# Moving the convolution accumulators of a decoder block into PSUM, and the layer-norm matmuls two gate chunks earlier

## The reference

```python
h  = RMSNorm(x)
u  = h @ w_in        # conv a, conv gate, q, k, v, indexer q, k, weights, branch gates
c  = a * sigmoid(gate)                      # 512 channels
c  = causal_depthwise_conv(c, width=31) + conv_b
c  = silu(LayerNorm(c)) @ w_conv_out        # branch A
y  = sparse_attention(top 256 keys of an indexer, 8 heads, ALiBi) @ w_attn_out   # branch B
x  = x + (sigmoid(g_A) * c + sigmoid(g_B) * y) @ w_out
x  = x + SwiGLU(RMSNorm(x));   out = RMSNorm(x)
```

## Time and profile before

| | us |
|---|---|
| median of 3 runs (lowest, highest) | 3663.2 (3662.07, 3664.06) |
| time of the profiled execution | 3664.39 |
| its span, first to last instruction | 3662.6 |
| PE busy | 3306.2 |
| DVE busy | 2275.9 |
| ACT busy | 1225.0 |
| POOL busy | 717.3 |

### The profile page before, as it was taken

The page is one execution under the profiler, slowest core; times in us unless marked ns, Lnnn a source line. Parts: engine busy times, 40 slices in busy tenths (PEclk is TensorE's granted clock), DMA queues, the critical chain, the costliest instruction groups (busy, mean ns, idle before and its releaser), DMA issues.

```text
span 3662.6 us, 42966 instructions
## 1 busy us (share of the span) xinstructions
PE 3306.2 (90%) x15365; PEld 2699.9 (74%) x15365; DVE 2275.9 (62%) x4000; ACT 1225.0 (33%) x2407; POOL 717.3 (20%) x482
## 2 busy tenths in 40 slices
PE   6971699999998899989999889998999978889998
PEld 5851578768887788758887778875788857768886
DVE  2968735678704935679972973667999988720001
ACT  3321542242334731251112763226211156621111
POOL 3420120026766100002112300000112231002112
PEclk9986799999999999999999999999999989999999
DMA  6951275559996165535555016552555510155554
GB/s 219 309 173 35 104 276 188 191 189 291 290 289 227 65 251 189 180 117 194 195 195 190 24 74 237 194 179 87 184 195 195 199 43 7 59 208 194 195 195 167
DMA packets 177571, 640.20 MB, mean 175 GB/s; under 512 B 11293, under 2 KB 95305, under 8 KB 115560
## 3 DMA queue, kind: packets, MB, share of 16 engines
q1 hardware_dynamic: 160512, 574.66, 45.4%
q10 hardware_dynamic: 16872, 63.01, 4.5%
HBM read 476.14 MB, written 161.48 MB: 174 GB/s over the span
## 4 chain that ended last, share of the span: by engine, by line
PE 62%; DVE 18%; issue 13%; ACT 3%; DMA 2%; POOL 1%; DVEq 0%; ACTq 0%; SPq 0%; POOLq 0%
PE PS L1346 13%; PE PS L1317 12%; PE PS L1319 12%; PE PS L1318 12%; DVE flags L1113 2%; DVE part_max L1200 2%; PE PS L1331 2%; DVE W L1098 1%; PE PS L1332 1%; PE PS L1333 1%; DVE PT L1212 1%; PE PS L1459 1%; PE PS L1504 1%; DVE ties L942 1%; DVE W L1212 1%
## 5 line engine op out<-in xcount | busy, mean ns | idle before, releaser
L1113 DVE TENSOR_SCALAR_CACHE_REDUCE flags<-W,cand 128x1408 uint8<-128x1408 f32 (+3 forms) x462 | 683.4, 1479 | 53.7 <-DVE cand L1143 40.0
L1346 PE MATMUL PS<-WS,HT 128*128 128x512 f32 x2088 | 481.8, 390 | 5.6 <-POOL WS L427 3.3
L1346 PEld LDWEIGHTS PS<-WS,HT 128*128 128x128 f32 x2088 | 392.9, 188 | 88.5 <-issue 4.1
L1317 PE MATMUL PS<-HF,WS 128*128 128x512 f32 x1072 | 419.8, 392 | 16.1 <-issue 13.8
L1318 PE MATMUL PS<-HF,WS 128*128 128x512 f32 x1072 | 419.2, 391 | 0.0
L1319 PE MATMUL PS<-HF,WS 128*128 128x512 f32 x1072 | 419.0, 391 | 0.0
L498 POOL TENSOR_TENSOR TMP<-TMP 128x512 f32<-128x512 f32 x88 | 113.4, 1289 | 1554.7 <-ACT TMP L855 1554.7
L427 POOL TENSOR_TENSOR WS<-RAW,WS 128x1024 fp32r<-128x1024 f32 x116 | 281.5, 2427 | 654.6 <-ACT WS L570 620.5
L1317 PE MATMUL PS<-HT,WS 128*128 128x512 f32 x824 | 325.2, 395 | 0.0
L1319 PE MATMUL PS<-HT,WS 128*128 128x512 f32 x824 | 320.8, 389 | 0.0
L1318 PE MATMUL PS<-HT,WS 128*128 128x512 f32 x824 | 320.6, 389 | 0.0
(11 more groups left out here) (223 smaller groups left out, 6376.5 us busy)
## 6 DMA issues: line engine op xcount, KB each, us to landing
WS<-split_weights_scratch SPq DMA_DIRECT2D x234, 1024.0 KB, 4.8
split_weights_scratch<-WS SPq DMA_DIRECT2D x116, 1024.0 KB, 5.0
W<-split_weights_scratch SPq DMA_DIRECT2D x114, 1024.0 KB, 4.8
RAW<-in_w_in SPq DMA_DIRECT2D x34, 512.0 KB, 6.0
RAW<-in_w_ffn_gate SPq DMA_DIRECT2D x22, 512.0 KB, 6.3
RAW<-in_w_ffn_up SPq DMA_DIRECT2D x22, 512.0 KB, 6.3
RAW<-in_w_ffn_down SPq DMA_DIRECT2D x22, 512.0 KB, 5.7
W<-in_x ACTq DMA_DIRECT2D x4, 2048.0 KB, 12.3
```

The source lines that it names most:

```text
L1113: step(nc.vector.tensor_scalar(flags[:, 0:n], SC[:, t, 0:n], cand[:, t:t + 1].bitcast(f32), 0.0, op, ALU.add, accum_out=count[:, t:t + 1]))
L1317: mm(PS[:, bank, :], wh, src[:, 0, k, :], start=k == 0, stop=False)
L1346: ins = mm(PS[:, 2 * t + half, :], lhs, split(c, w_part)[:, half * 512:(half + 1) * 512], start=first and part == 0 and w_part == 0, stop= ...
```

## The change

The convolution's accumulator of each 128 channels moves from SBUF into one of the PSUM banks 4 to 7 (`TAPSUM`). Only the last tap writes to `ACC` in SBUF. All projections now share banks 0 to 3: queries in a ring of four, gate B in a ring that starts at bank 2, the key/value transposes in banks 2 and 3, gate A in a ring of two (banks 0 and 1), mean and variance in banks 2 and 3. In `taps` and in the first tap (L1018) `ACC` becomes `TAPSUM` in the same way as in `tap`. Waits follow the banks. `LN_MEAN` and `LN_VAR` become 3 and 5, so the two products are issued ahead of gate-A chunks 3 and 5, and ACT's squares and square root come after its gates 2 and 4. The number of instructions does not change.

```diff
-    LN_MEAN, LN_VAR = 5, 7
+    LN_MEAN, LN_VAR = 3, 5
+        TAPSUM = PS[:, 4:8, :]
...
-            def tap(k):
+            def tap(k, out):
...
-                    nc.vector.scalar_tensor_tensor(out=ACC[:, c, :], in0=GLU[:, c, k:k + ROWS], scalar=cw[:, c, k:k + 1],
-                                                   in1=ACC[:, c, :], op0=ALU.mult, op1=ALU.add).then_inc(conv_step, 1)
+                    nc.vector.scalar_tensor_tensor(out=out[:, c, :], in0=GLU[:, c, k:k + ROWS], scalar=cw[:, c, k:k + 1],
+                                                   in1=TAPSUM[:, c, :], op0=ALU.mult, op1=ALU.add).then_inc(conv_step, 1)
...
-                        tap(1 + j)
+                        tap(1 + j, TAPSUM)
...
-                    taps(TAPS - 8, TAPS)
+                    taps(TAPS - 8, TAPS - 1)
+                    tap(TAPS - 1, ACC)
...
-                    for j in range(N_Q):
-                        pe.wait_ge(q_free, (N_Q + 2) * g + j + 1)
-                        col_chunk(c0 + A_Q + j, 4 + j % 4, HT)
+                    for u in range(4):
+                        pe.wait_ge(glu_done, KC * g + (3 if u < 2 else 4))
+                        col_chunk(c0 + A_Q + u, u, HT)
+                    for u in range(4):
+                        pe.wait_ge(q_free, (N_Q + 2) * g + u + 5)
+                        col_chunk(c0 + A_Q + 4 + u, u, HT)
...
-                    pe.wait_ge(glu_done, KC * (g + 1))
                     for d in range(KD):
-                        if d >= 4:
+                        if d < 4:
+                            pe.wait_ge(q_free, (N_Q + 2) * g + 4 + N_Q - 1 + d)
+                        else:
                             pe.wait_ge(gb_stage, KD * g + d - 3)
-                        col_chunk(c0 + A_GB + d, d % 4, HT)
+                        col_chunk(c0 + A_GB + d, (d + 2) % 4, HT)
                     pe.wait_ge(kv_copied, 2 * (g + 1))
-                    pe.wait_ge(q_free, 4 + (N_Q + 2) * (g + 1))
+                    pe.wait_ge(gb_stage, KD * g + KD - 2)
...
                     for d in range(KD):
-                        if d < 4:
-                            pe.wait_ge(gb_stage, KD * g + d + 5)
+                        if d < 2:
+                            pe.wait_ge(gb_stage, KD * g + d + 7)
                         else:
-                            pe.wait_ge(gate_free, KD * g + d - 3)
+                            pe.wait_ge(gate_free, KD * g + d - 1)
...
-                        col_chunk(c0 + A_GA + d, d % 4, HT)
+                        col_chunk(c0 + A_GA + d, d % 2, HT)
```

More of the change, by code:

```diff
@@ L655, in _ @@
                             scale = 2.0 ** (h + 1) * DH ** -0.5 if j < 4 else 1.0
-                            nc.scalar.activation(dst[0:DH, h, :], PS[DH * e:DH * e + DH, 4 + j % 4, :], ACT.Copy,
+                            nc.scalar.activation(dst[0:DH, h, :], PS[DH * e:DH * e + DH, j % 4, :], ACT.Copy,
                                                  scale=scale).then_inc(q_hi, 1)
@@ L661, in _ @@
                         for e in range(2):
-                            nc.scalar.activation(dst[DH * e:DH * e + DH, ROWS * g:ROWS * g + ROWS], PS[0:DH, 4 + j, :],
+                            nc.scalar.activation(dst[DH * e:DH * e + DH, ROWS * g:ROWS * g + ROWS], PS[0:DH, j, :],
                                                  ACT.Copy).then_inc(q_hi, 1)
-                        nc.scalar.activation(TMP[:, 2 + j, :], PS[:, 4 + j, :], ACT.Copy,
+                        nc.scalar.activation(TMP[:, 2 + j, :], PS[:, j, :], ACT.Copy,
                                              scale=1.0 if j == 0 else HEADS ** -0.5).then_inc(kv_copied, 1)
@@ L674, in _ @@
                             act.wait_ge(gb_out[s], 16 * n_before)
-                        nc.scalar.activation(TMP[:, s, :], PS[:, d % 4, :], ACT.Sigmoid,
+                        nc.scalar.activation(TMP[:, s, :], PS[:, (d + 2) % 4, :], ACT.Sigmoid,
                                              bias=vcol[:, V_BG + KD + d:V_BG + KD + d + 1]).then_inc(gb_stage, 1)
@@ L681, in _ @@
                     nc.scalar.activation(VV[:, RT * g:RT * g + RT, 0, :],
-                                         PS[:, 4, :].rearrange("p (t d) -> p t d", t=RT)[:, :, DH:2 * DH], ACT.Copy).then_inc(v_hi, 1)
+                                         PS[:, 2, :].rearrange("p (t d) -> p t d", t=RT)[:, :, DH:2 * DH], ACT.Copy).then_inc(v_hi, 1)
                     for d in range(KD):
@@ L685, in _ @@
                         used(c)
-                        nc.scalar.activation(SGA[:, d, :], PS[:, d % 4, :], ACT.Sigmoid,
+                        nc.scalar.activation(SGA[:, d, :], PS[:, d % 2, :], ACT.Sigmoid,
                                              bias=vcol[:, V_BG + d:V_BG + d + 1]).then_inc(gate_free, 1)
@@ L984, in taps @@
                         dve.wait_ge(conv_step, KC * conv_n - KC + c + 1 + KC * i)
-                        nc.vector.scalar_tensor_tensor(out=ACC[:, c, :], in0=GLU[:, c, ds(k0 + i, ROWS)],
-                                                       scalar=cw[:, c, ds(k0 + i, 1)], in1=ACC[:, c, :], op0=ALU.mult,
+                        nc.vector.scalar_tensor_tensor(out=TAPSUM[:, c, :], in0=GLU[:, c, ds(k0 + i, ROWS)],
+                                                       scalar=cw[:, c, ds(k0 + i, 1)], in1=TAPSUM[:, c, :], op0=ALU.mult,
                                                        op1=ALU.add).then_inc(conv_step, 1)
@@ L1017, in _ @@
                     for c in range(KC):
-                        nc.vector.tensor_scalar(ACC[:, c, :], GLU[:, c, 0:ROWS], cw[:, c, 0:1],
+                        nc.vector.tensor_scalar(TAPSUM[:, c, :], GLU[:, c, 0:ROWS], cw[:, c, 0:1],
                                                 vcol[:, V_CB + c:V_CB + c + 1], ALU.mult, ALU.add).then_inc(conv_step, 1)
@@ L1026, in _ @@
                             dve.wait_ge(q_hi, (2 * N_Q + 4) * g + 2 * j + e + 1)
-                            ins = nc.vector.scalar_tensor_tensor(out=dst[DH:2 * DH, h, :], in0=PS[DH * e:DH * e + DH, 4 + j % 4, :],
+                            ins = nc.vector.scalar_tensor_tensor(out=dst[DH:2 * DH, h, :], in0=PS[DH * e:DH * e + DH, j % 4, :],
                                                                  scalar=scale, in1=dst[0:DH, h, :].bitcast(f32), op0=ALU.mult,
@@ L1036, in _ @@
                             cols = slice(ROWS * g, ROWS * g + ROWS)
-                            ins = nc.vector.tensor_tensor(out=lo_t[DH * e:DH * e + DH, cols], in0=PS[0:DH, 4 + j, :],
+                            ins = nc.vector.tensor_tensor(out=lo_t[DH * e:DH * e + DH, cols], in0=PS[0:DH, j, :],
                                                           in1=hi_t[0:DH, cols].bitcast(f32), op=ALU.subtract)
@@ L1043, in _ @@
                     dve.wait_ge(v_hi, g + 1)
[L1044 removed]
+                    nc.vector.tensor_copy(wi[:, :, :], PS[:, 3, :].rearrange("p (t d) -> p t d", t=RT)[:, :, DH:DH + HEADS])
                     nc.vector.tensor_tensor(out=VV[:, RT * g:RT * g + RT, 1, :],
[L1046 removed]
+                                            in0=PS[:, 2, :].rearrange("p (t d) -> p t d", t=RT)[:, :, DH:2 * DH],
                                             in1=VV[:, RT * g:RT * g + RT, 0, :].bitcast(f32), op=ALU.subtract).then_inc(v_ready, 1)
[L1048 removed]
+                    taps(TAPS - 8, TAPS - 1)
+                    tap(TAPS - 1, ACC)
                     dve.wait_ge(conv_step, KC * conv_n)
@@ L1053, in _ @@
                     for c in range(KC):
-                        nc.vector.tensor_tensor(out=ACC[:, c, :], in0=ACC[:, c, :], in1=PS[:, 6, :],
+                        nc.vector.tensor_tensor(out=ACC[:, c, :], in0=ACC[:, c, :], in1=PS[:, 2, :],
                                                 op=ALU.subtract).then_inc(xc_ready, 1)
                     dve.wait_ge(var_psum, g + 1)
-                    nc.vector.tensor_scalar(TMP[:, 0, :], PS[:, 7, :], LN_EPS, None, ALU.add).then_inc(ln_sqrt, 1)
+                    nc.vector.tensor_scalar(TMP[:, 0, :], PS[:, 3, :], LN_EPS, None, ALU.add).then_inc(ln_sqrt, 1)
                     dve.wait_ge(ln_sqrt, 2 * g + 2)
@@ L1410, in _ @@
                             for c in range(KC):
-                                ins = mm(PS[:, 6, :], meanm[:, :], ACC[:, c, :], start=c == 0, stop=c == KC - 1)
+                                ins = mm(PS[:, 2, :], meanm[:, :], ACC[:, c, :], start=c == 0, stop=c == KC - 1)
                             ins.then_inc(mean_psum, 1)
@@ L1415, in _ @@
                                 pe.wait_ge(sq_done, KC * g + c + 1)
-                                ins = mm(PS[:, 7, :], meanm[:, :], TMP[:, c, :], start=c == 0, stop=c == KC - 1)
+                                ins = mm(PS[:, 3, :], meanm[:, :], TMP[:, c, :], start=c == 0, stop=c == KC - 1)
                             ins.then_inc(var_psum, 1)
-                        col_chunk(c0 + A_GA + d, d % 4, HT)
+                        col_chunk(c0 + A_GA + d, d % 2, HT)
```

4 lines of the change are left out of this document (2 added, 2 removed).

## The result

The changed kernel takes 3677.1 us (median of 7 runs, 3674.9 to 3680.7) against 3664.1 for the kernel before (7 runs, 3662.1 to 3673.8). The ratio is 1.0032, 95% interval 1.002 to 1.0044: slower by 0.2 to 0.4%. PE's busy time is 3313.6 us, DVE's 2233.2.

What follows compares the result with a forecast made beforehand. PE was taken to hold most of the last-ending chain, DVE a fifth. Group 0's -15.6 us and groups 1 to 3's +24.4 gave net +8.8, so 3673 on the profiled execution and 3672 on the median; range 3663 to 3683.

Steps and rivals of the forecast that it cites:

- one net of two sums: Whole kernel: group 0 gains 15.6 us, groups 1 to 3 lose 24.4 together, net +8.8 us.
- Part 1: Convolution taps in group 0: with the accumulator in PSUM they run at the free pace, 0.664 us, ending at 199.5.
- Part 2: Mean two chunks earlier: PE's wait for the taps gains 13.1 us in group 0, loses 6.5 in each other group.
- part 5: Everything else, such as bank rings, waits, DMA order and weight rounding: taken at nothing.
- Part 3: PE's slower clock after idling before the mean: groups 1 to 3 lose 2.3 us each, group 0 regains 0.8.
- the lower bound: Smallest clock loss taken for PE after its idle before the mean: 1.8 us, against 3.1 at most.
- Part 4: Earlier layer norm before CO: nearly nothing, 0.68 us gained in each of groups 1 to 3, 1.75 in group 0.
- rival (a): Taps in PSUM cost more than in SBUF, pitch 0.70 to 0.745 us: 3677 to 3682 us, chance 0.17.
- (b): POOL still holds the taps in group 0, which end at 223.5 as before: 3697 us, chance 0.05.
- (c): Taps in PSUM are cheaper: pitch 0.60 us gives 3664, 0.53 gives 3655; chance 0.13, of which faster 0.08.

Runs made afterwards that it cites:

- the last run: Changed kernel with mean and variance ahead of chunks 4 and 6, one more tap before the key/value wait, Silu ahead of gate 7: 3625.7 us, 0.9886 against the kernel before.
- the other kernel with taps in SBUF: Kernel before with only mean and variance moved ahead of gate-A chunks 3 and 5, taps and banks as before: 3693.2 us, ratio 1.0075.

## Why the prediction was right

The forecast was 3672 us, slower, by one net of two sums; it came out 3677, in the range, with the sign. The sums on the record against the traces:

| | forecast | measured |
|---|---|---|
| group 0, wait for the mean | 20.0 to 6.9 | 19.99 to 7.07 |
| groups 1 to 3, wait | 6.4 each | 6.27, 6.27, 6.63 |
| mean matmuls beyond 3.59 | 2.3 each | 2.0, 1.5, 2.8, 3.1 |
| Silu's wait for DVE | gone, 0.68 and 1.75 gained | gone; the stall in front of CO is 0.84 shorter in each of groups 1 to 3 and 1.91 in group 0 |
| group 0, sum | -15.6 | -12.0 |
| groups 1 to 3, sum | +24.4 | +25.5 |

**Part 1** (free taps in group 0) held: pitch 0.660 against 0.664. That L1027, with one operand in PSUM, never was delayed was the row that told it. **Part 2** held to 0.3 us in each group: the end of the taps hangs on the key/value transposes, PE's arrival too, so both shift together. The 5.0 us by which 32 taps exceed three chunks are not the whole of the 6.3: the copies and the hand-overs around them are the rest, which the forecast had through its marks and not through that difference. Its absolute marks for group 0 were 4 us early (taps ended at 199.5 there, at 203.4 in the trace); see part 5. **Part 3** held in its mean, 2.3 against 2.36, while single groups lie between 1.5 and 3.1, below the lower bound once; that the mean came so close is partly luck. **Part 4** was the one on which the sign hung: without it one would book 5 to 7 us a group for the stall that a layer norm two chunks earlier should remove. The row with 0.68 us of idle in front of the Silu showed that DVE was late by only so much; the run with ACT's order turned showed what does hold most of it.

**Part 5** is where the sum was short. The tap in PSUM costs no more: a pitch of 0.660 us against 0.664, and 743 ns against 747, so rival (a) falls. The Trainium skill, page "Perfetto Trace Analysis", section "Optimizing Scalar/DVE Operations", gives an overhead of about 60 ns on SBUF and 125 on PSUM, by which 128 awaited taps would be 8.3 us longer, as an estimate; the trace doesn't agree for this instruction. But weights at "nothing" were not nothing in group 0. PE's wait for the low part of the weights, which is not among its waits before, ACT's timeline with a rounding that waits for its weights, and the value copy:

```profile
PE PS L1320 <- POOL WS L429: 2.6, 2, 1.5
...
170.00 1.06 ACT L572 ACTIVATE WS<-RAW 128x1024 fp32r<-128x1024 f32 x1 [2.12 <-DMA RAW<-in_w_in]
...
181.33 0.36 ACT L683 ACTIVATE VV<-PS 128x256 fp32r<-128x256 f32 x1
```

The value copy is read at 181.33, before at 177.34: 0.65 from an earlier start and 3.35 in gate B, where ACT waited for weights from DRAM. In that stretch (135 to 175) the DMA engines are busy 0.99 before and 0.89 here. Without these 4.0 us group 0's own terms hold: -12.9 (wait), -1.1 (clock) and -1.9 (stall in front of CO) are -15.9 against the forecast's -15.6.

Why the weights came later is open. Five kernels with the same code up to there (the changed one and the runs with positions 5 and 7, 4 and 6, the added matmuls, and ACT's order turned) show 46.95, 44.34, 45.12, 44.96 and 44.64 us from the low parts of the indexer key to the value copy. Two that differ from them only in how many taps DVE does there show 45.28 (two more taps) and 47.44 (one more), and the two with taps in SBUF 43.61 and 45.49. So the same code scatters by 2.6 us, in a stretch in which the DMA engines are nearly always busy. But all seven with taps in PSUM are longer than the kernel before, by 0.7 to 3.8 us, so a part that belongs to the change isn't excluded. What the change does there is to free POOL too: its instruction for the low parts (L427, now L429) took up to 3009 ns before and 2498 at most after, so the buffers of the weights come free at other times. Nothing was run that holds these apart. Nor does the record show this stretch for the other six executions: their times, 3674.9 to 3680.7 us, are no shorter as a whole than the profiled 3676.5, so the scatter of one execution doesn't explain why the median is 13.0 above the kernel before and not 8.8.

The net was put at 8.8 with 7.3 as the bound of what can be told, and the measured 12 to 13 is above it: the sign is clear of noise, and clearer than the forecast could know. One outcome can't test the chances. Rivals (b) and (c) fall with the pitch and the maximum of L987.

## What to carry to other kernels

A consumer moved earlier must be checked against the last producer that can't move: compare what each engine has left from their common event on (here 21.3 us of taps, and the copies ahead of them, against 16.3 us of chunks), not the idle time that the profile shows elsewhere. Two edits that come together can have opposite signs; here one gained 19 us (3645.9 against 3664.8 beside it) and the other lost 31 (3677.1 against 3645.9). And before booking a stall as removed, look at the idle time of each link of its chain: the link with no idle holds it, here ACT's program order. When that link is mended, look again: in group 0 of the last run DVE had become the link that comes last.

## What the runs showed of the hardware

- A DVE instruction with one operand in SBUF and one in PSUM is untouched by POOL (maximum 751 ns over 336 taps), while the same with two in SBUF reached 2904 in the loop. The Trainium skill, page "SBUF — State Buffer", section "Who interferes with whom", says that a DVE instruction with at most one SBUF input, outside the 2-port performance modes, doesn't contend with GpSimd; the trace agrees, with these numbers.
- The delay went both ways. POOL's instruction for the low parts, before and after (ns, min/median/max):

```profile
L427 POOL TENSOR_TENSOR WS<-RAW,WS x116: 2338/2397/3009, 6.3 to 1143.8; 128x1024 fp32r<-128x1024 f32 x116
...
L429 POOL TENSOR_TENSOR WS<-RAW,WS x116: 2340/2398/2498, 6.3 to 1138.7; 128x1024 fp32r<-128x1024 f32 x116
```

The longest is 2814 ns in the other kernel with taps in SBUF, and 2487 to 2631 in the six others with taps in PSUM.

- Accumulating in place in a PSUM bank is as fast as in SBUF: 743 ns and a pitch of 0.660 us, against 747 and 0.664.
- Stops of PE of 0.7 to 2.0 us ahead of the mean left the clock at full, twelve of twelve (eight matmuls in 3.67 to 3.70 us). In front of CO, six stops of 1.5 to 1.6 us did too, but one of 1.87 us was followed by half of the clock from 240.2 to 243.7, so the length of a stop alone doesn't settle it. The stops of 3.66 us and more at these two places were all followed by half of it: for 2.8 to 6.1 us behind the four of 6.3 to 7.1 us in the changed kernel. A longer stop didn't cost more: behind 25.3 us the eight mean matmuls took 5.55 us, behind 20.0 us 6.66. The same stop (6.27 us, twice) cost 1.5 us once and 2.8 the other time.
